# The high part of a feed-forward branch's input stands 0 to 864 bytes further from the weight pieces

## What is computed

```python
def swiglu(x, w_in, w_out):
    gate, up = jnp.split(x @ w_in, 2, axis=-1)      # w_in 1024 x 5632, w_out 2816 x 1024
    return (jax.nn.silu(gate) * up) @ w_out

for layer in range(4):
    h = h + 0.5 * rmsnorm(swiglu(rmsnorm(h, g[0]), ffn_w_in[layer, 0], ffn_w_out[layer, 0]), g[1])
    ...                                             # the mixer
    h = h + 0.5 * rmsnorm(swiglu(rmsnorm(h, g[4]), ffn_w_in[layer, 1], ffn_w_out[layer, 1]), g[5])
```

## Time and profile before

| | us |
|---|---|
| median of 3 runs | 3418.73 |
| the profiled execution | 3408.6 |
| its span, first to last instruction | 3406.8 |
| TensorE busy with matmuls | 3239.8 |
| VectorE busy | 1961.1 |
| ScalarE busy | 1516.6 |
| GpSimd busy | 178.6 |

### The profile page before, as it was taken

How to read it: one execution, slowest core, us unless ns; L and a number is a source line. 1 busy time by engine, 2 the same in 40 slices (tenths; PEclk the granted TensorE clock), 3 DMA queues, 4 the chain that set the end, 5 groups by cost and what they waited for, 6 DMA issues and landing times.

```text
span 3406.8 us, 49232 instructions
## 1 busy us (share of the span) xinstructions
PE 3239.8 (95%) x21142; PEld 2854.5 (84%) x21142; DVE 1961.1 (58%) x2964; ACT 1516.6 (45%) x2538; POOL 178.6 (5%) x201
## 2 busy tenths in 40 slices
PE   6998999999999999998999989999999999999898
PEld 6987998978898987696989978987878887887797
DVE  4557555557555555674555565555456555825777
ACT  4446444454445443213444455454544344524554
POOL 0000000003000000230000000000011000100100
PEclk9999999999999999998999999999999999999999
DMA  6563656555556544414556554551013333531452
GB/s 228 186 203 106 210 186 225 189 169 178 192 189 224 188 157 149 136 44 150 190 180 211 191 173 155 186 181 28 26 62 112 123 125 125 178 93 62 132 190 99
DMA packets 411239, 522.01 MB, mean 153 GB/s; under 512 B 41575, under 2 KB 353500, under 8 KB 410892
## 3 DMA queue, kind: packets, MB, share of 16 engines
q1 hardware_dynamic: 405980, 516.23, 46.1%
q0 software_dynamic: 816, 2.10, 0.2%
q10 hardware_dynamic: 4224, 0.52, 0.1%
HBM read 516.19 MB, written 2.10 MB: 152 GB/s over the span
## 4 chain that ended last, share of the span: by engine, by line
PE 86%; DVE 7%; ACT 4%; issue 1%; DMA 1%; POOL 0%; SPq 0%; DVEq 0%; ACTq 0%; POOLq 0%
PE ps L186 24%; PE ps L188 23%; PE ps L187 23%; PE ps L178 5%; PE ps L196 2%; PE ps L1226 2%; DVE fast_xt L716 1%; ACT a L1246 1%; DVE small L1283 1%; PE ps L559 1%; PE ps L1938 1%; PE ps L3802 0%; PE ps L3799 0%; DVE tmp L646 0%; DVE a L1279 0%
## 5 line engine op out<-in xcount | busy, mean ns | idle before, releaser
L186 PE MATMUL ps<-a 128*128 128x256 f32 (+1 forms) x4832 | 1519.1, 314 | 37.2 <-DVE fast_xt L716 15.9
L188 PE MATMUL ps<-a 128*128 128x256 f32 (+1 forms) x4664 | 1456.2, 312 | 0.0
L186 PEld LDWEIGHTS ps<-a 128*128 128x128 f32 x4832 | 914.9, 189 | 100.9 <-DVE fast_xt L716 15.3
L187 PE MATMUL ps<-fast_xt,a 128*128 128x256 f32 x3400 | 958.3, 282 | 0.0
L188 PEld LDWEIGHTS ps<-a 128*128 128x128 f32 x4664 | 887.1, 190 | 52.1
L892 DVE TENSOR_TENSOR a<-ring,a 128x1024 fp32r<-128x1024 f32 x594 | 693.5, 1221 | 348.5 <-ACT a L886 348.5
L886 ACT ACTIVATE a<-ring 128x1024 fp32r<-128x1024 f32 x594 | 586.4, 1049 | 232.3 <-PE ps L188 231.4
L187 PEld LDWEIGHTS ps<-fast_xt,a 128*128 128x128 f32 x3400 | 645.3, 190 | 7.4
L187 PE MATMUL ps<-a 128*128 128x512 f32 (+1 forms) x1368 | 527.3, 385 | 0.0
L187 PEld LDWEIGHTS ps<-a 128*128 128x128 f32 x1368 | 257.8, 188 | 43.3
L990 ACT ACTIVATE tmp<-ps 128x256 f32<-128x256 f32 x176 | 67.6, 384 | 487.0 <-PE ps L188 487.0
(11 more groups left out here) (378 smaller groups left out, 3850.7 us busy)
## 6 DMA issues: line engine op xcount, KB each, us to landing
ring<-in_ffn_w_in_dram SPq DMA_DIRECT2D x220, 1024.0 KB, 7.5
ring<-in_ffn_w_out_dram SPq DMA_DIRECT2D x121, 1024.0 KB, 5.0
ring<-in_ada_w_dram SPq DMA_DIRECT2D x48, 1024.0 KB, 5.5
ring<-in_swa_w_qkv_dram SPq DMA_DIRECT2D x12, 1024.0 KB, 8.1
ring<-in_gla_w_in_dram SPq DMA_DIRECT2D x12, 1024.0 KB, 6.9
ring<-in_rwkv_w_rkv_dram SPq DMA_DIRECT2D x12, 1024.0 KB, 5.2
ring<-in_na_w_qkv_dram SPq DMA_DIRECT2D x12, 1024.0 KB, 5.2
ring<-in_swa_w_o_dram SPq DMA_DIRECT2D x8, 1024.0 KB, 5.5
```

The lines of the kernel that those rows point to most:

```text
L186: pe.x.matmul(out, lh, rh, start=start and i == 0, stop=False)
L187: pe.x.matmul(out, lh, rl, start=False, stop=False)
L188: ins = pe.x.matmul(out, ll, rh, start=False, stop=stop and i == n - 1)
```

## The change

A table gives for each branch how many elements (4 bytes) are put ahead of the weight pieces and between them and the room of the input's high part. The first number is 0 everywhere. The spare room behind the high part is made smaller by as much. Branches 0 and 10 are not in the table. With the rounding to 32 bytes, `xh` stands further by 32 (branch 1), 64 (2), 128 (3), 256 (4), 512 (5), 864 (6) and 32 bytes (7); in branch 7, whose 16 bytes and 8176 bytes are both rounded up, `ht` and `hs` stand 32 bytes further as well.

```diff
+PLACE = {1: (0, 8), 2: (0, 16), 3: (0, 32), 4: (0, 64), 5: (0, 128), 6: (0, 216), 7: (0, 4)}
+
+
 def ffn_memory(K, f, w_in, w_out):
     c = Core()
     c.w_in, c.w_out = w_in, w_out
+    ahead, between = PLACE.get(f, (0, 0))
+    if ahead:
+        K.arena(ahead)
     c.pieces = [(K.arena(1024, F32R), K.arena(1024, F32R)) for _ in range(6)]
+    if between:
+        K.arena(between)
     c.xs = v3(K.arena(2048, F32R), T), v3(K.fast_xt[:, 0:2048], T)
-    K.arena(2048)
+    K.arena(2048 - ahead - between)
     c.ht = [K.arena(T) for _ in range(2)]
     c.hs = [(K.arena(T, F32R), K.arena(T, F32R)) for _ in range(LATE)]
```

## The result

The changed kernel takes 3422.63 us (median of 20 runs, 3418.41 to 3433.37), the kernel before 3415.12 us beside it (20 runs, 3409.07 to 3424.73): 1.0025 times as long, 95% interval 1.0017 to 1.0033. The medians are 7.5 us apart. I had forecast 8.3 us less. The profiled execution took 3423.1 us.

A forecast was written before the change was run, and what follows sets the result against it. TensorE's own stream was taken as the bound. Branch 6 at -4.8 us, branch 5 at 0 and branches 1 to 4 and 7 at -3.5 gave -8.3: 3418.7 to 3410.4 us; likeliest range 3402 to 3417, all cases 3388 to 3428.

The forecast's parts named there:

- What bounds the kernel: Whole kernel: TensorE has matmuls running for 95% of 3406.8 us; its own stream's rate changes a feed-forward branch one for one.
- I cost this at nothing: Ahead of a branch: ScalarE copies and VectorE subtraction using the high part, at most about 0.3 us a branch, taken as 0.
- The low step's price: 256-wide steps streaming `fast_xt` (L187): 113.1 ns if high steps cost 120.0; branch 6 was to get it, -4.8 us.
- The lowest price for three that some steady stretch did reach: Branches 1 to 4 and 7, 256-wide steps: 351.2 ns for three, 0.7 us saved each, -3.5 us together.
- Branch 5 and its reason: High part 512 bytes further looks like the same place, since weights at 288 and 800 show one price: 0 us.
- The 12 steps of 512 must stay at 2.73: End of each column: the 512-wide steps keep 2.73 us in all branches except perhaps 7, whose weights move.
- Rival 1: Branches' streamed operands: place inside a kilobyte is nothing, room or neighbours explain the differing rows; 3418.7 us, chance 0.27.
- Rival 2: High part and weights at the same place cost; any other distance saves 4.8 us in six branches; 3389.9 us, chance 0.18.
- Rival 3: At some distances streamed operand and weights hinder each other: high steps 5.0 ns longer, 3.5 us a branch; 3428, chance 0.16.
- Rival 4: Rounding makes branches 1 and 7 the same, moves of 32 to 256 bytes too small; only branch 6 gains; 3413.9, chance 0.09.
- below 353.1: Three 256-wide steps cost 353.1 ns before; forecast 339.3 in branch 6, 351.2 in branches 1 to 4 and 7; chance 0.30.
- The rule: TensorE's separate read ports for streamed operand and weights: by it the sum would be 0 instead of -8.3 us.

## Why the prediction was wrong

**What bounds the kernel: right.** The sum of 22 columns over seven branches gives the whole effect, with no other engine in it, and the run with high and low part alike shows it one for one (29.1 us from the columns, 28.8 measured).

**"I cost this at nothing" (the copies, the subtraction, the spare room): right.** With moves by multiples of 256 the ratio is 1.0005.

**The low step's price: the step that failed.** From rows 8 I took 120.0 ns for a high step and put the rest of 353.1 on the low one: 113.1. The first half was nearly right, the high steps by themselves cost 119.8. But the low step by itself costs 120.1, not 113.1; it was the alternation of the two distances, 0 and 96, that was 6.6 ns cheap for three. A price was given to one step that belonged to the three together. The timeline of before could have told: over branch 2 the time from a start to the next averages 117.9 ns behind a high step (L186), 117.5 behind a low one (L187) and 117.8 behind the other high one (L188), and behind low steps it always lies between 116 and 120. One of them:

```profile
573.24 0.28 PE L187 MATMUL ps<-fast_xt,a 128*128 128x256 f32 x1
573.36 0.28 PE L188 MATMUL ps<-a 128*128 128x256 f32 x1
```

So branch 6, which I moved onto the place of the low step to get 339.3 for three, lost the alternation and got 5762/16 = 360.1, three times the low step's own price. Expected -4.8 us, measured +3.2: 8 of the 16 us between forecast and result lie in this one term.

**"The lowest price for three that some steady stretch did reach" for branches 1 to 4 and 7: wrong in sign.** -0.7 us each, measured +1.0, +1.5, +0.9, 0 and +1.8. I took the price of rows 10, a mix with other operands, for places that no row shows. Of the eight distances open to the high part the one before has the cheapest column.

**Branch 5 and its reason: right.** Rows 8 showed one even price for weights at 288 and at 800, 512 apart. The period is in fact 256, which makes branch 4 free too.

**"The 12 steps of 512 must stay at 2.73": wrong.** They take 33 to 41 ns more in branches 1, 2 and 6 with all their operands in place, and 61 in branch 7. In branch 6 the first ten take 1843.14 - 1840.83 = 2.31 us where before they took 2.27; the last ones run as before. The 512-wide steps settle at 226.7 ns in both, but how soon depends on the 256-wide steps before them, and the other way round: with only the hidden activations moved the 48 steps go up to 5.662. What is carried over stays open. This is the part that I had put at nothing: 0.7 to 0.9 us a branch in 1, 2 and 6.

```profile
1843.14 0.39 PE L187 MATMUL ps<-a 128*128 128x512 f32 x1
```

**The rivals.** Rival 1 (place is nothing) fell. Rival 2 had the high part at the weights' place as the cost; by itself that distance is dear (119.8), but with the low part 96 off it is the best there is. Rival 3 came nearest: distances between streamed operand and weights, as a lasting property of a branch, at which steps are dearer. Its 3.5 us a branch hold for branch 6 (3.2), the others cost a quarter to a half of that, but five branches of six cost something, and its 3428 is 5 us from the result. Its mechanism, each high step 5.0 ns longer, is not what the cycles show. Rival 4 fell with branch 1, where 32 bytes cost 47 ns a column, and branches 1 and 7 are not the same: `hs` makes 33 ns between them. I had given rival 3 0.16 and put "below 353.1" ahead of it on one subtraction and on rows 10. Every steady 256-wide row but one (rows 10) was above it.

**The rule.** The Trainium skill, SBUF — State Buffer, section "Who interferes with whom", gives TensorE two independent read ports, one for the streamed operand and one for weights. By that the distance between them could cost nothing; measured, it moves a 256-wide step between 116.8 and 120.1 ns and a 512-wide one between 227.5 and 233. The measurement decides.

## What to carry to other kernels

A price found by subtracting one step's price from a mix is no price of the other step: read the times between the starts of single steps first, and run each kind alone before moving anything onto it. Where TensorE is the bound and loads weights at each step, write down the addresses modulo 256 of what it streams and of what it loads, and expect up to 2.6% of the stream's time from their distances. The same place for streamed operand and weights was the cheapest at 512 columns and a dear one at 256. Move rooms by multiples of 256 where nothing is to change. And compare the granted clock of the whole program after any gain of that size: 10.5 us won in the branches were no measured gain in the whole, and time at half clock alone differs by 13 us between the profiled executions of before (116 us) and of the moves by multiples of 256 (129 us), whose columns are the same.

## What the hardware showed that I had not expected

- The rate of a matmul stream depends on distances modulo 256 bytes, in most branches to the ns over 18 columns and at other absolute addresses: 8.327 to 8.547 us a column, 2.6%.
- The steps of such a stream run through a cycle, in most places between 112 and 125 ns from start to start, with a mean of 116.7 to 120.0 ns; at the same addresses one column averaged 118.9 ns a step and the next 117.7.
- Behind the 256-wide steps, 512-wide ones with weights and streamed operand at one place took none to eleven steps to settle at 226.7 ns: 2.719 us for twelve at the cheapest column, 2.807 with l = 64 and x = 128.
- The clock can fall to half for 181 us while TensorE is busy for 180.25 of them. It fell after dense 512-wide steps had given way to the small matmuls of the neighbourhood attention, with 0.78 us of idle between:

```profile
3068.87 0.40 PE L188 MATMUL ps<-r,fast_xt 128*128 128x512 f32 x1
...
3070.05 0.70 PE L3799 MATMUL ps<-a 64*128 64x256 f32 x2 [0.78 <-DVE a L3880]
...
3072.93 1.22 PE L3802 MATMUL ps<-ring,cst 128*128 128x256 f32 x2
```

  The Trainium skill, TensorE: Matmul & The Clock Gate, section "What's actually happening", has activity release the throttle. Here a stream that the records show as busy all the time stayed at half clock until the next phase. What in the layout makes this likely wasn't found.
